# Small experts by fetched rows in place of dense products over both tables

## The reference

```python
def peer_ffn(u, w_q, sub_keys, u_tab, v_tab):          # T=256, H=8, K=16, D=1024
    q = (xt @ w_q).reshape(T, H, 2, PEER_DKEY // 2)
    s = jnp.einsum('thcd,hcnd->thcn', q, sub_keys)      # two sets of 128 keys a head
    top_s, top_i = lax.top_k(s, K)
    cand = (top_s[:, :, 0, :, None] + top_s[:, :, 1, None, :]).reshape(T, H, K * K)
    cand_i = (top_i[:, :, 0, :, None] * PEER_NKEYS + top_i[:, :, 1, None, :]).reshape(T, H, K * K)
    best_s, best_j = lax.top_k(cand, K)
    expert = jnp.take_along_axis(cand_i, best_j, axis=-1)
    g = jax.nn.softmax(best_s, axis=-1)
    # per chunk of 128 tokens
    act = jax.nn.gelu(jnp.einsum('cd,chkd->chk', xc, u_tab[ec]), approximate=False)
    return jnp.einsum('chk,chkd->cd', gc * act, v_tab[ec])
```

## Time and profile before

| | us |
|---|---|
| median of 3 runs | 1823.0 (1822.63 to 1825.28) |
| profiled execution | 1819.45 |
| its span | 1817.2 |

### The profile page before, as it was taken

The page is one execution under the profiler, slowest core; times in us unless marked ns, Lnnn a source line. Parts: engine busy times, 40 slices in busy tenths (PEclk is TensorE's granted clock), DMA queues, the critical chain, the costliest instruction groups (busy, mean ns, idle before and its releaser), DMA issues.

```text
span 1817.2 us, 29118 instructions
## 1 busy us (share of the span) xinstructions
PE 1745.8 (96%) x11932; PEld 1407.2 (77%) x11932; DVE 907.0 (50%) x1792; ACT 684.0 (38%) x1157; POOL 320.9 (18%) x301
## 2 busy tenths in 40 slices
PE   8999999999999899999989999999999999999997
PEld 7777555555555499665878999999999988888885
DVE  4543111111111343664535899666666455656765
ACT  4620100010000244554344444555555444444443
POOL 0000000000000000000003420244443133444342
PEclk8999999999999999999999999999999999999998
DMA  7219999999999736221523387756555877777774
GB/s 316 93 68 418 424 424 424 424 424 425 425 424 424 324 120 237 88 94 55 224 93 128 101 227 227 225 175 176 177 174 174 237 247 235 236 234 235 235 236 138
DMA packets 99656, 443.67 MB, mean 244 GB/s; under 512 B 10432, under 2 KB 43712, under 8 KB 79424
## 3 DMA queue, kind: packets, MB, share of 16 engines
q1 hardware_dynamic: 99088, 440.59, 67.3%
q10 hardware_dynamic: 432, 1.18, 0.2%
HBM read 423.91 MB, written 17.83 MB: 243 GB/s over the span
## 4 chain that ended last, share of the span: by engine, by line
PE 87%; issue 6%; DVE 4%; ACT 2%; DMA 1%; POOL 0%; SPq 0%; DVEq 0%; ACTq 0%; POOLq 0%
PE PS L191 85%; PE PS L201 2%; DMA CO<-in_const 1%; DVE AR L845 1%; DVE XL L261 0%; DVE Wk L843 0%; DMA CO<-g_hold 0%; DVE LO L187 0%; ACT XH L254 0%; ACT AR L1618 0%; ACT Wk L1313 0%; DVE NTs L274 0%; DVE AR L274 0%; DVE Wk L274 0%; ACT HI L180 0%
## 5 line engine op out<-in xcount | busy, mean ns | idle before, releaser
L1826 DVE TENSOR_TENSOR TL<-Wk,TH 128x1024 fp32r<-128x1024 f32 x256 | 338.0, 1321 | 196.8 <-ACT TH L1809 196.7
L191 PE MATMUL PS<-XH,TH 128*128 128x256 f32 x1024 | 295.2, 288 | 0.8 <-DVE TL L1826 0.8
L191 PE MATMUL PS<-XL,TH 128*128 128x256 f32 x1024 | 289.6, 283 | 0.0
L191 PE MATMUL PS<-XH,TL 128*128 128x256 f32 x1024 | 289.6, 283 | 0.0
L1809 ACT ACTIVATE TH<-Wk 128x1024 fp32r<-128x1024 f32 x256 | 268.1, 1048 | 0.0
L191 PE MATMUL PS<-AR 128*64 128x256 f32 (+2 forms) x1912 | 202.8, 378 | 0.7 <-DVE FL L835 0.7
L191 PE MATMUL PS<-TH,WH 128*128 128x512 f32 x512 | 202.6, 396 | 0.0
L191 PE MATMUL PS<-TH,WL 128*128 128x512 f32 x512 | 202.6, 396 | 0.0
L191 PE MATMUL PS<-TL,WH 128*128 128x512 f32 x512 | 202.6, 396 | 0.0
L191 PEld LDWEIGHTS PS<-XH,TH 128*128 128x128 f32 x1024 | 196.2, 192 | 1.0 <-DVE TL L1826 1.0
L191 PEld LDWEIGHTS PS<-XL,TH 128*128 128x128 f32 x1024 | 196.4, 192 | 0.0
(11 more groups left out here) (277 smaller groups left out, 2783.2 us busy)
## 6 DMA issues: line engine op xcount, KB each, us to landing
Wk<-in_peer_u SPq DMA_DIRECT2D x128, 512.0 KB, 3.8
Wk<-in_peer_v SPq DMA_DIRECT2D x128, 512.0 KB, 4.4
AR<-in_w_gate SPq DMA_DIRECT2D x28, 2048.0 KB, 12.7
AR<-in_w_up SPq DMA_DIRECT2D x27, 2048.0 KB, 14.1
AR<-in_w_down SPq DMA_DIRECT2D x27, 2048.0 KB, 14.7
AR<-in_w_in SPq DMA_DIRECT2D x15, 2048.0 KB, 9.8
CO<-g_hold SPq DMA_DIRECT2D x128, 128.0 KB, 4.3
g_hold<-RW SPq DMA_DIRECT2D x86, 128.0 KB, 3.7
```

What stands on the lines that cost most here:

```text
L191: return pe.matmul(o, l, r, start=start, stop=stop, skip_group_check=True)
L1826: dve.tensor_tensor(TL[:, i % 5], RAW[:, i % 5], TH[:, i % 3].bitcast(F32), ALU.subtract).then_inc(*lows_made.up())
```

## The change

The dense stage is gone. The two tables lie side by side in one input `uv` of 16384 rows of 2048 (8 KB a row). For each of the 128 pairs of a token and each half of the tokens there is one indirect DMA, issued by GpSimd, which fetches for 128 tokens the row that each has chosen, 256 in all, into a ring of 14 slots. VectorE makes the dot of each token with its u part (`dots`, four fetches a batch), the token's scaled state being in two banks of PSUM. ScalarE takes the Gelu, multiplies by the gate, and writes the weights of the 128 tokens on a diagonal. PE multiplies the diagonal with the v part in two products of 512 columns, in plain float32, and adds up over the 128 pairs in PSUM.

Selection is done for one half of the tokens and one unit at a time (8 groups n of 32 fetches), with `dots` between its steps, and wholly on VectorE; group 0 comes right after its keys. The low parts of pq3 move from GpSimd to VectorE, behind group 0. PE does batch 0 between units 2 and 3. The query and key steps have two banks each instead of four. The first half of the tokens is finished during the second.

```diff
+        RING = [Wk[:, 0:2048], Wk[:, 2048:4096], *(AR[:, 2048 * k:2048 * k + 2048] for k in range(12))]
+        ROUND = [*range(8, 14), 4, 5, 6, 7, 0, 1, 2, 3]
+        place_of = [g if g < 8 else g - 8 if g < 12 else ROUND[(g - 12) % 14] for g in range(256)]
...
+        def add_rows_pe(pe, b):
+            for g in range(4 * b, 4 * b + 4):
+                tt, n = g // 128, g % 128
+                pe.wait_ge(diags, g + 1)
+                for j in range(2):
+                    t = mm(pe, sums_at(tt, j), DG[:, g % 8, :], RING[place_of[g]][:, 1024 + 512 * j:1536 + 512 * j], n == 0, n == 127)
+                t.then_inc(summed, 1)
...
             for ui in range(4):
-                lows = c_dve if ui < 2 else p_pool
+                lows = (c_dve, c_dve, p_pool, p_dve)[ui]
                 for m in range(4):
...
+                    if hc >= 2:
+                        pe.wait_ge(*p_act.at(f"q{hc - 2}"))
...
                 keys(hc)
+                if ui == 2:
+                    add_rows_pe(pe, 0)
+            for b in range(1, 64):
+                add_rows_pe(pe, b)
+        def weights_act(act, b):
+            cs = slice(4 * b, 4 * b + 4)
+            act.wait_ge(dotted, b + 1)
+            act.activation(GEL[:, cs], DT[:, cs], ACT.Gelu).then_inc(*a_own.up())
+            if b % 8 == 0:
+                act.wait_ge(*p_dve.at(f"gates{b // 8}"))
+            act.wait_ge(*a_own.at())
+            for g in range(4 * b, 4 * b + 4):
+                t = act.activation(WT[:, g:g + 1], BGf[:, g:g + 1], ACT.Copy, scale=GEL[:, g:g + 1])
+            t.then_inc(*a_own.up())
+            act.wait_ge(*a_own.at())
+            for g in range(4 * b, 4 * b + 4):
+                if g >= 8:
+                    act.wait_ge(summed, g - 7)
+                act.activation(DG[:, g % 8, :], ident, ACT.Copy, scale=WT[:, g:g + 1]).then_inc(diags, 1)
+        def exp_act(act, n):
+            v = group_of(BG, n)
+            act.wait_ge(*p_dve.at(f"sub{n}"))
+            act.activation(v, v, ACT.Exp).then_inc(*p_act.up(f"exp{n}"))
...                                                            # peer_act, in its loop over ui
+                if ui == 1:
+                    exp_act(act, 0)
                 if ui == 2:
-                    high(act, 0)
-                    high(act, 1)
+                    weights_act(act, 0)
+            for b in range(1, 64):
+                if b in DOTTED_AT_SUB:
+                    exp_act(act, DOTTED_AT_SUB.index(b))
+                weights_act(act, b)
...
+        def dots(dve):
+            b = batches.count
+            for g in range(4 * b, 4 * b + 4):
+                r = RING[place_of[g]][:, 0:1024]
+                dve.wait_ge(g_in[place_of[g]], 16 * uses[g])
+                t = dve.tensor_tensor_reduce(r, r, P(6 if g < 128 else 2, 2), 1.0, 0.0, ALU.mult, ALU.add, DT[:, g:g + 1])
+            t.then_inc(*batches.up())
+        def select(dve, n, early, late):
+            tt, ui = n // 4, n % 4
+            a0, hs = tt * 16 + 4 * ui, slice(2 * ui, 2 * ui + 2)
+            for half in range(2):
+                if tt == 0:
+                    dve.wait_ge(*p_act.at(f"key{4 * ui + 2 * half + 1}"))
+                top16(dve, S, TS, TIi, [a0 + 2 * half, a0 + 2 * half + 1], (nothing, late)[half])
+                if half == 0:
+                    early(dve)
...                                                            # the 50 sums, seven additions
+            dve.tensor_copy(TF[:, a0:a0 + 4, :], TIi[:, a0:a0 + 4, :]).then_inc(*own.up())
+            early(dve)
...
+            top16(dve, CA, BS, BJ, [h0, h0 + 1], nothing)
...                                                            # the key numbers, as before, 512 wide
+            dve.scalar_tensor_tensor(IDX[:, 32 * n:32 * n + 32], I1, 128.0, I2, ALU.mult, ALU.add).then_inc(*p_dve.up(f"idx{n}"))
...
+            tokens_dve(dve, 0)
+            select(dve, 0, nothing, nothing)
+            gates(dve, 0)
+            low_quarters(dve, "pq3", p_act, p_dve)
+            dots(dve)
+            for n in range(1, 8):
+                select(dve, n, dots, dots if n > 1 else nothing)
+                dots(dve)
+                gates(dve, n)
...
+            while batches.count < 64:
+                dots(dve)
...
         def peer_pool(pool):
             low_quarters(pool, "pq2", p_act, p_pool)
-            low_quarters(pool, "pq3", p_act, p_pool)
...
+            for g in range(256):
+                if g % 32 == 0:
+                    pool.wait_ge(*p_dve.at(f"idx{g // 32}"))
+                if g in (2, 6, 12):
+                    pool.wait_ge(*p_pe.at({2: "q7", 6: "q11", 12: "q15"}[g]))
...
+                if earlier[g] is not None:
+                    pool.wait_ge(summed, earlier[g] + 1)
+                k = place_of[g]
+                pool.indirect_dma_start(RING[k], None, uv, bass.IndirectOffsetOnAxis(ap=IDX[:, g:g + 1], axis=0)).then_inc(g_in[k], 16)
```

More of the change, by code:

```diff
@@ L274, in scaled @@
             return dve.tensor_scalar(o, i, s, None, ALU.mult)
-        rms = Steps(sem("rms"), ["half", "x", "vg", "mix", "ffn", "end1", "nmix", "o", "mem", "cross", "small", "end2"])
+        rms = Steps(sem("rms"), ["half", "x", "vg", "mix", "ffn", "end1", "nmix", "o", "mem", "cross", "small", "end2a", "end2b"])
         HALF = ST[:, 32:40]
@@ L1800, in peer_act @@
                 keys(hc)
+                if ui == 1:
+                    exp_act(act, 0)
                 if ui == 2:
-                    high(act, 0)
-                    high(act, 1)
[L1805 to L1826, removed]
+                    weights_act(act, 0)
[3 more added lines that the diff above has]
+                weights_act(act, b)
+            act.wait_ge(*e_dve.at("h10"))
+            square_sum(act, H[:, 1, 0:512], JUNK[:, 0:512], ST[:, 41:42]).then_inc(*e_act.up("sq"))
         def top16(dve, src, vals, idx, rws, between):
@@ L1844, in top16 @@
                     dve.wait_ge(*own.at())
[L1846 to L1854, removed]
@@ L1886, in column_keys @@
[L1886 to L1893, removed]
+        batches = Own(dotted)
+        def dots(dve):
[5 more added lines that the diff above has]
+            t.then_inc(*batches.up())
@@ L1961, in peer_dve @@
-            assert lows_made.count == LOWS_BEFORE_SUB, lows_made.count
-            dve.tensor_tensor(BG, BS, bc(BS[:, :, 0:1], [128, 16, 16]), ALU.subtract).then_inc(*p_dve.up("sub"))
-            for _ in range(3):
-                low(dve)
-            dve.wait_ge(*p_act.at("exp"))
-            dve.tensor_reduce(gs[:, 0, :], BG, AX, ALU.add).then_inc(*own.up())
-            dve.wait_ge(*own.at())
-            dve.reciprocal(gs[:, 1, :], gs[:, 0, :]).then_inc(*own.up())
-            dve.wait_ge(*own.at())
@@ new lines, in peer_dve @@
+            dve.wait_ge(summed, 128)
+            for j in range(2):
+                added(dve, 0, j)
+            dve.wait_ge(*e_dve.at("h01"))
+            square_sum_dve(dve, H[:, 0, :], JUNK, ST[:, 40:41]).then_inc(*e_dve.up("ss0"))
+            dve.wait_ge(*e_dve.at("ss0"))
+            mean(dve, ST[:, 40:41], D).then_inc(*e_dve.up("mean0"))
+            while batches.count < 64:
+                dots(dve)
+                if batches.count == SCALED_AT:
+                    dve.wait_ge(*rms.at("end2a"))
+                    dve.wait_ge(ld_fin, 16)
+                    dve.scalar_tensor_tensor(FO[:, 0], H[:, 0, :], ST[:, 40:41], NTs[:, 0:1024], ALU.mult, ALU.mult).then_inc(
+                        *e_dve.up("out0"))
@@ new lines, in peer_dve @@
+            dve.wait_ge(summed, 256)
+            for j in range(2):
+                added(dve, 1, j)
+            dve.wait_ge(*e_dve.at("h11"))
+            square_sum_dve(dve, H[:, 1, 512:1024], JUNK[:, 512:1024], ST[:, 42:43]).then_inc(*e_dve.up("ss1"))
+            dve.wait_ge(*e_act.at("sq"))
+            dve.wait_ge(*e_dve.at("ss1"))
+            dve.tensor_tensor(ST[:, 41:42], ST[:, 41:42], ST[:, 42:43], ALU.add).then_inc(*e_dve.up("sum1"))
+            dve.wait_ge(*e_dve.at("sum1"))
+            mean(dve, ST[:, 41:42], D).then_inc(*e_dve.up("mean1"))
@@ L1972, in peer_pool @@
+            dve.wait_ge(*rms.at("end2b"))
+            for j in range(2):
+                ns = slice(512 * j, 512 * j + 512)
+                dve.scalar_tensor_tensor(FO[:, 1, ns], H[:, 1, ns], ST[:, 41:42], NTs[:, ns], ALU.mult, ALU.mult).then_inc(
+                    *e_dve.up(f"out1{j}"))
         def peer_pool(pool):
```

404 lines of the change are left out of this document (112 added, 292 removed).

## The result

The changed kernel takes 1683.4 us (median of 4 runs, 1683.0 to 1684.5) against 1822.8 for the kernel before: a ratio of 0.9237, 95% interval 0.9226 to 0.9248, 139 us less. The forecast was 1681 us, with a range of 1640 to 1890. The profiled execution took 1684.5 us; its span is 1682.7.

The account below looks back on a forecast made before the run. It took TensorE to bound the old dense stage (785 us) and transfers the new one. Start 1045 + 244 gathers x 2.5 + end 22.5 = 1677.5 us of span, about 1681 us as time; range 1640 to 1890.

Parts of the forecast that it names:

- The bound: New gather stage: transfers are the bound, with DMA share near 1.0 and 410 to 425 GB/s from about 1045 us.
- The likeliest case: Whole kernel: transfers bound the new stage at 2.5 us a gather, about 1681 us in all; chance 0.66.
- The pace: Gather stream: 2.5 us for each 1.049 MB gather, bounds 2.37 and 3.71 us.
- The issue: GpSimd issuing gathers: between 0.38 and 2.4 us each, hidden behind the gather before.
- The engines: Gather stream, per gather: PE 1.75 us, VectorE's dot 1.23 us, ScalarE under 4 us of 10 per batch of four.
- The check on the middle stretch: VectorE during selections: 24 dots of 1.23 us and an 18 us selection take 48 us, against 60 for 24 gathers.
- The start: Before the steady stream: indices at 1000, q11 at 1018, q15 frees gather 12's slots about 1045 us; bounds 1030 to 1055.
- The ring: Slots held from issue to sum: 18 us chain against 35 us for 14 slots, so transfers stay the bound.
- The term for the last landing: End of the gather stream: the last gather lands 3 us after the pace, within the 22.5 us end.
- the last step: From span to time: 2.25 us around the span, median of the runs 3.5 above that; 1677.5 became about 1681.
- The slow gather: Rival in the gather stream: chance addresses or GpSimd's issue make gathers slower than 3.07 us each; chance 0.22.
- VectorE as the bound: Rival during selections: dots of 2.3 us make 3.05 us a gather, 88 us more, 1769 us; chance 0.10.

Follow-up runs that it names:

- half the bytes: Against the changed kernel, gathers fetch 4 KB rows of peer_u alone and both products read that half: 1495.2 us.
- half the products: Against the changed kernel, PE makes one product of 512 columns for each row in place of two, still with 8 KB rows: 1677.9 us.
- rows in line: Against the changed kernel, each gather reads one whole stretch of 1 MB in place of the chosen rows: 1680.6 us.
- the run with the low parts on VectorE: Against the changed kernel, only the low parts of pq2 move from GpSimd to VectorE, ahead of group 0's seven additions: 1681.4 us.
- the run with seven: Against the changed kernel, GpSimd issues gather g only when gather g - 7 has been added up, so 7 are held, not 14: 1834.6 us.

## Why the prediction was right

**The bound.** Named, and shown by three runs: half the bytes give 188 us, half the products nothing in the stream, rows in line nothing. The likeliest case was the one that came.

**The pace.** 2.5 us a gather was taken, 2.49 measured. The row that carried it was the stage of the big experts, since a third of its loads had 8 KB rows. The other end of the bound, 283 GB/s from 4 KB rows, was a poor reading: a share of 0.81 can't be scaled up to a full one. With 4 KB rows in a deep queue the engines moved 362 GB/s at a share of 0.96.

**The issue.** Between 0.38 and 2.4 us was the bound; 0.94 us and a gap of 0.30 measured. With 1.24 us it is hidden. By estimate from these two figures it would be up to 845 GB/s (1.0486 MB in 1.24 us).

**The engines.** PE was put at 1.75 us a gather and needs 1.70 in a full stretch, but in the changed kernel it is busy 1.93 us a gather, since its clock is not full (below). The dot was put at 1.23, and 1.14 is what back-to-back dots take. PSUM as its second operand cost nothing. The check on the middle stretch (48 of 60 us) was too high, on the safe side: from 1100 to 1300 VectorE is busy 145.7 of 200 us, which is 44 of 60.

**The start.** Indices at 1000 predicted, 1003 measured. The keys that it waits for came 3.6 us later than in the kernel before. GpSimd's norm step was already 2.2 us later (963.25 against 961.07); 0.3 us of that is ScalarE's two issues of the keys' load (1.4 us against 1.1), and the rest was there before them. The other 1.4 us came behind it, while the chip granted a lower clock (0.83 at 960 to 970, 1.00 before). The collision of the earlier trace rows was read rightly: 7.49 us for seven additions. The Trainium skill (SBUF — State Buffer, Who interferes with whom) has it that a VectorE instruction with two SBUF operands and a GpSimd instruction that reads SBUF exclude each other; the run with the low parts on VectorE agrees, 0.67 us. PE stood 4.7 us for group 0's exp, not 7, and its clock fell as forecast. q11 at 1016 (1018 predicted), q15 at 1042.3 (1045), and ahead of it the idle gap of the DMA engines that was forecast, with a share of 0.00 from 1040 to 1042.

**The ring.** The reason given was right, and nearly the size: 14 slots hold 35 us; the chain was put at 18, and by the run with seven it is some 21.7. That run lies past the edge; no depth between 7 and 14 was tried. VectorE's longest stretch without a dot is 9.6 us from one dot to the next (9 predicted).

**What was mis-sized.** The term for the last landing, 3 us beside 244 gathers of 2.5. From the issue at 1042.3 to the landing at 1662.9 are 620.6 us, so beside 244 x 2.5 the term measured 10.6, and 13.0 beside 2.49. Two pieces make it. The first gather after the pause takes 8.4 us from issue to landing, 5.9 more than its turn of 2.49. And the last lands 7.1 us after 1050.7 + 243 x 2.49 = 1655.8. There the rows of the result section show one DMA engine of 16 at work until 1662.45, and the last landings are 2.46 us apart, which is the time of this engine for its eight packets of each gather (8 x 0.31). Why one engine is behind the others no run shows. With seven in flight, or with half rows, this tail is missing. Start 2.7 us early, stream and landings 7.6 us late, end (19.8 us after the landing, 19.5 predicted) 0.3 us late: together the 5.2 us between 1677.5 and the span.

**Luck in the last step.** From the span to the time the prediction adds 3.5 us, but its own figures give 2.25 + 3.5 = 5.8, so the sum should have read 1683.3. Measured, the median lies 0.7 us above the profiled span. The number is 2.4 us off because 5.2 us too few in the span met 2.8 too many here; with the sum done right the forecast would have met 1683.4, and that too by errors that cancel.

**The rivals.** The slow gather: its threshold of 3.07 us lay 0.58 us away, and the run with seven in flight went over it and was slower than the kernel before. VectorE as the bound: not here; but with half the bytes it has no idle time during selections. The clock: forecast near 1.00, since PE would stand only 3 us a batch; that reason did not hold. PE stands about 2.8 us before most batches and, behind VectorE's long stretch, 5.8 once a group:

```profile
1366.59 5.27 PE L189 MATMUL PS<-AR 128*128 128x512 f32 x8 [5.79 <-ACT AR L1819]
1371.69 3.60 PE L189 MATMUL PS<-Wk,AR 128*128 128x512 f32 x8
...
1665.77 8.83 PE L189 MATMUL PS<-AR 128*128 128x512 f32 x16 [2.71 <-ACT AR L1819]
```

After 5.8 us the first two rows take 5.27 us at a clock of 0.69, the next two 3.60 at 1.00. After 2.7 to 2.9 us four rows take 7.13 us at full clock or, as at the end, 8.83 at 0.81. In the stream this costs nothing, as argued and as the run with one product shows; at the end it costs 1.7 us.

## What to carry to other kernels

Where a dense product is bound by PE and the rows that matter are few, count bytes and nothing else first: 256 gathers of 1 MB at 421 GB/s replace 785 us of products by 638 us of transfer, though they move more bytes than the whole tables hold. Such a stream is worth its full rate only if the ring covers the whole chain from issue to release; work the chain out, here some 20 us, before choosing the depth. Then look at the two ends: what gates the first slots, and how many products stand behind the last landing.

## What the runs showed of the hardware

An indirect gather of 128 rows keeps GpSimd 0.94 us, with 0.30 us to the next, for rows of 8 KB and of 4 KB alike. Rows of 8 KB at chance addresses move at 421 GB/s, those in line too; rows of 4 KB at 362 GB/s, at a share of 0.96. A gather of 1 MB takes 8.4 us from issue to landing after a pause, and with at most seven in flight 5.4 at the least and 7.8 in the median. At the end of a full stream of 8 KB rows one DMA engine of 16 was some 7 us behind the others, and the last gathers landed with it. Issues beside VectorE's low parts, which have two SBUF operands, took 1.6 to 2.0 us in place of 0.94, and moved with them when these came earlier.
